# Two attention stages of a decoder step merged into one stage with a shared clock of 328 ticks

## The reference

```python
D_MODEL, SEQ, DEC_BATCH, DEC_SEQ, PAST_LEN, PAGE_SIZE = 1024, 2048, 8, 4, 4096, 128
HEAD_DIM, W_ATTN, N_HEADS_A = 64, 512, 8

def stick_breaking_block(q, k, v, bias, q_pos, k_pos):
    z = jnp.einsum('bqhd,bkhd->bhqk', q, k) * (HEAD_DIM ** -0.5) + bias[None, :, None, None]
    causal = k_pos[None, :] < q_pos[:, None]
    log_1m_beta = jnp.where(causal, jax.nn.log_sigmoid(-z), 0.0)
    tail = lax.cumsum(log_1m_beta, axis=3, reverse=True) - log_1m_beta
    w = jnp.where(causal, jnp.exp(jax.nn.log_sigmoid(z) + tail), 0.0)
    return jnp.einsum('bhqk,bkhd->bqhd', w.astype(v.dtype), v)

def attend_sample(q, k, v, bias, l=l):
    k_past = cache_k[l][page_table].reshape(n_seq_s, past_len, N_HEADS_A, HEAD_DIM)
    v_past = cache_v[l][page_table].reshape(n_seq_s, past_len, N_HEADS_A, HEAD_DIM)
    keys = jnp.concatenate([k_past, k], axis=1)
    vals = jnp.concatenate([v_past, v], axis=1)
    return stick_breaking_block(q, keys, vals, bias, past_len + jnp.arange(t_new), jnp.arange(past_len + t_new))
```

## Time and profile before

| what | us |
|---|---|
| median of three executions | 3194.71 |
| the profiled execution | 3192.91 |
| its span, first to last instruction | 3191.4 |
| prompt attention, 727.4 to 1298.2 | 570.8 |
| sample attention, 1298.2 to 1735.3 | 437.1 |

### The profile page before, as it was taken

One profiled execution on the slowest core, in us unless ns is written; L12 is line 12 of the kernel. 1 busy time (PEld: TensorE's weight loads), 2 busy tenths in 40 slices (PEclk: granted clock), 3 DMA queues, 4 the chain that ended last, 5 costly groups with the idle time before them and its releaser, 6 DMA issues. The chain is left out here.

```text
span 3191.4 us, 46062 instructions
## 1 busy us (share of the span) xinstructions
PE 2709.6 (85%) x15013; PEld 1384.8 (43%) x15013; DVE 1380.4 (43%) x2512; ACT 937.2 (29%) x1751; POOL 503.0 (16%) x678
## 2 busy tenths in 40 slices
PE   7999999977888888687776999679999999899940
PEld 3444444423444444344442455335554554455520
DVE  3141413237999999333321777612221221122237
ACT  2313030216888888222221122110100000001014
POOL 0101010100000000133332122211111111111136
PEclk9999999988999999899997999889999999999975
DMA  7020101066131510599996343378796669968637
GB/s 296 13 79 23 70 27 40 27 259 202 50 124 63 160 40 1 185 351 349 333 345 190 137 148 126 119 236 271 244 313 200 207 205 338 359 217 277 230 107 252
DMA packets 275565, 575.30 MB, mean 180 GB/s; under 512 B 59210, under 2 KB 75659, under 8 KB 271168
## 3 DMA queue, kind: packets, MB, share of 16 engines
q1 hardware_dynamic: 192620, 427.99, 38.6%
q0 software_dynamic: 82480, 145.43, 14.1%
q10 hardware_dynamic: 324, 0.10, 0.0%
HBM read 460.86 MB, written 112.29 MB: 180 GB/s over the span
## 5 line engine op out<-in xcount | busy, mean ns | idle before, releaser
L1930 PE MATMUL h<-w,xT 128*64 128x256 f32 x5120 | 590.7, 384 | 15.4 <-DMA w<-in_w 14.1
L1930 PEld LDWEIGHTS h<-w,xT 128*64 128x64 f32 x5120 | 363.9, 138 | 239.1 <-issue 70.6
L968 DVE TENSOR_TENSOR_SCAN left<-leave,left 128x512 f32<-128x512 f32 (+3 forms) x320 | 356.7, 1115 | 30.6 <-ACT leave L931 30.5
L418 PE MATMUL bank<-xnT,w_in 128*128 128x512 f32 x768 | 330.3, 592 | 0.0
L1943 PE MATMUL yb<-w,hT 128*64 128x512 f32 x1280 | 310.2, 606 | 0.0
L1010 PE MATMUL tb<-ident,w 128*128 128x128 f32 x1088 | 178.4, 288 | 88.1 <-DVE w L959 86.2
L1911 ACT ACTIVATE sg<-h 128x128 f32<-128x128 f32 x160 | 44.4, 278 | 687.0 <-PE h L1930 687.0
L1590 PE MATMUL pb<-w_out,featT 128*128 128x512 f32 x512 | 229.4, 601 | 2.3 <-DVE t L1655 2.3
L418 PEld LDWEIGHTS bank<-xnT,w_in 128*128 128x128 f32 x768 | 145.6, 190 | 181.8 <-issue 180.3
L931 ACT ACTIVATE leave<-zb,nbiasP 128x512 f32<-128x512 f32 (+3 forms) x320 | 208.4, 651 | 40.8 <-DVE w L959 27.6
L418 PE MATMUL bank<-w_in,xnT 128*128 128x512 f32 x512 | 220.4, 592 | 0.0
(11 more groups left out here) (366 smaller groups left out, 2886.9 us busy)
## 6 DMA issues: line engine op xcount, KB each, us to landing
w<-in_w SPq DMA_DIRECT2D x96, 2048.0 KB, 20.3
vp<-in_cache_v POOLq DMA_DIRECT2D x256, 256.0 KB, 5.1
w<-in_cache_k SPq DMA_DIRECT2D x256, 256.0 KB, 4.8
ys_d<-zeros SPq DMA_DIRECT2D x32, 816.0 KB
slab<-in_w_ada SPq DMA_DIRECT2D x24, 1024.0 KB, 18.3
ys_d<-y POOLq DMA_DIRECT2D x83, 256.0 KB, 10.0
x_in<-xs_d POOLq DMA_DIRECT2D x162, 128.0 KB, 6.2
w_in<-in_w_in SPq DMA_DIRECT2D x5, 2048.0 KB, 20.3
```

What stands on the lines that cost most here:

```text
L418: mm = pe.matmul(ps[:, :], w, m, start=(i == 0), stop=(i == len(parts) - 1))
L968: dve.tensor_tensor_scan(left[n % 4][:, at:at + cols][:, ::-1], leave[n % 4][:, 0:cols][:, ::-1], leave[n % 4][:, 0:cols][:, ::-1], left[n ...
L1930: mm = pe.matmul(h[half][q * G:q * G + G, 0:2 * P], xT[:, c % (XW // P), c // (XW // P) * G:c // (XW // P) * G + G], w13[i][:, c, :, cols] ...
```

## The change

`attention_phase` takes the place of both stages. PE, ACT and DVE walk one list of ticks, n = 0 to 327. At tick n PE turns item n-2 and, in the same three banks `tb`, one of 16 pieces of the sample group's K, ACT and DVE copy what was turned the tick before, ACT makes the sigmoids of item n, and DVE the product of item n-1 and the scan of item n. The sample group's units are windows of 19 ticks from tick 3: K pieces at positions 0 to 15 of a window, new positions' scores at 16, the unit's scores at 17 (in a `tb` bank), its scan at 18, the turned weights at 2 of the next window and the V products in quarters at 4, 7, 10 and 13.

In detail:
- `zb` has three banks instead of four; `tb` is shared by everything that is turned and by the sample scores; `kb` is gone.
- ACT and DVE make their copies ahead of the sigmoids and the scan of a tick, and DVE the product of n-1 ahead of the scan of n.
- The scan of an item gets its start value from a one-column copy or memset (`first`), issued after the scan of the item before; `left` is 512+1 columns, and the product is written over `take`.
- The K copies are 13 by ACT and 3 by DVE per unit, the weight copy is ACT's.
- K has two buffers of 4 pages, V two buffers of one position of all four sequences (4 pages); a V buffer is free when its quarter of products is done.
- The zero fills are issued by SP behind every second group of 4 K pages.
- `rowsS` and `rowsP` are loaded by POOL at the start of the router, since K uses their place before.

```diff
+    FIRST, WINDOW, TICKS = 3, 19, N + 8
+    def place(n):
+        return divmod(n - FIRST, WINDOW) if n >= FIRST else (-1, 0)
...
-        zb = [k.ps(f"zb{i}", [P, GRP]) for i in range(4)]
+        zb = [k.ps(f"zb{i}", [P, GRP]) for i in range(3)]
+        kp = [k.sb(f"kp{i}", [P, PPC, WA]) for i in range(2)]
+        vp = [k.sb(f"vp{i}", [P, 4, WA]) for i in range(2)]
+        kTs = [keep["rows_mem"][j // 2][:, 2 * (j % 2):2 * (j % 2) + 2, :].rearrange("p a (b n) -> p (a b) n", n=CH) for j in range(4)]
...
+                for u in range(NU):
+                    for j in range(4):
+                        g = 4 * u + j
+                        if g >= 2:
+                            turned(sp, "k_turn", (g - 2) // 4, 4 * ((g - 2) % 4) + FC - 1)
+                        page(sp, "cache_k", kp[g % 2], s_kp[g % 2], u, j)
+                        if g == 1:
+                            new_rows(0)
+                            load(1)
+                            sp.wait_ge(s_set, 1)
+                        if j == 1:
+                            zero_rows(2 * u)
+                        if j == 3:
+                            zero_rows(2 * u + 1)
...
+                for g in range(PPC * NU):
+                    u, i = divmod(g, PPC)
+                    if g >= 2:
+                        pool.wait_ge(s_spv, g - 1)
+                    for j in range(4):
+                        at = (4 * (u // NY) + j) * NPAGES + (NY - 1 - u % NY) * PPC + i
+                        number = pool.value_load(pages[0:1, at:at + 1], min_val=0, max_val=NPHYS - 1)
+                        pool.dma_start(vp[g % 2][:, j, :], cache["cache_v"][ds(number, 1)].rearrange("a p n -> (a p) n")).then_inc(s_vp[g % 2], 16)
...
+                for n in range(TICKS + 1):
+                    if n % 4 == 2 and 8 <= n < N:
+                        outputs(n // 4 - 2)
+                    if 0 <= n - 3 < N and (n - 3) % 4:
+                        turn(n - 3)
+                    u, p = place(n - 1)
+                    if p == 2 and 1 <= u <= NU:
+                        w_turn(u - 1)
+                    if p < 4 * FC and p not in (3, 7, 11) and 0 <= u < NU:
+                        k_turn(u, p)
...
+                    if n < N:
+                        pair, _, _, par, cols = item(n)
+                        head = 2 * pair + par
+                        act.wait_ge(s_z, n + 1)
+                        if n >= 4:
+                            act.wait_ge(s_sc, n - 3)
+                            turned(act, "turn", n - 4)
...
+                def first(n):
+                    _, t, c, _, cols = item(n)
+                    if n >= 4:
+                        dve.wait_ge(s_w, n - 3)
+                    if c == t // TPG:
+                        dve.memset(left[n % 4][:, cols:cols + 1], 1.0).then_inc(s_in, 1)
+                    else:
+                        dve.tensor_copy(left[n % 4][:, GRP:], left[n % 4][:, 0:1]).then_inc(s_in, 1)
+
+                def weights(n):
+                    cols = item(n)[4]
+                    dve.wait_ge(s_tk, n + 1)
+                    dve.wait_ge(s_sc, n + 1)
+                    dve.tensor_tensor(take[n % 4][:, 0:cols], take[n % 4][:, 0:cols], left[n % 4][:, 1:cols + 1], ALU.mult).then_inc(s_w, 1)
...
+                def free(*name):
+                    e = EVENT[name]
+                    if e >= 3:
+                        copied(pe, *EVENTS[e - 3][0])
+                    return bank(*name)
...
+                for n in range(TICKS):
+                    if n % 2 and n + 1 < N:
+                        scores((n + 1) // 4, (n + 1) % 4 // 2)
+                    if 2 <= n < N + 2:
+                        turn(n - 2)
...
+                    if p < 4 * FC and 0 <= u < NU:
+                        k_turn(u, p)
...
+                    if p == 17 and 0 <= u < NU:
+                        sample_scores(u)
+                    if 6 <= n < N + 6:
+                        values((n - 6) // 4, (n - 6) % 4)
+                    if p == 3 and u in (1, NY + 1):
+                        new_values(u // NY)
+                    if p in (4, 7, 10, 13) and 1 <= u <= NU:
+                        sample_values(u - 1, (p - 4) // 3)
...
+                pool.dma_start(keep["rowsS"][:, :, :], io["mod_d"][1:, :].unsqueeze(1).to_broadcast([BS, TS, 4 * D])).then_inc(s["rows"], 16)
+                pool.dma_start(keep["rowsP"][:, :, :], io["mod_d"][0:1, :].to_broadcast([P, 4 * D])).then_inc(s["rows"], 16)
...
                 dve.wait_ge(s["small"], 48)
+                dve.wait_ge(s["rows"], 32)
```

More of the change, by code:

```diff
@@ L822, in prompt_attention_phase @@
     N = 4 * M
-    LAG = 4
+    PPC = 4
+    CH = PPC * PAGE
+    NY = PAST // CH
+    NU = 2 * NY
+    FIRST, WINDOW, TICKS = 3, 19, N + 8
+    def place(n):
+        return divmod(n - FIRST, WINDOW) if n >= FIRST else (-1, 0)
+    EVENTS = []
+    for n in range(TICKS):
+        unit, p = place(n)
+        if 2 <= n < N + 2:
+            EVENTS.append((("turn", n - 2), "dve" if (n - 2) % 4 == 0 else "act"))
+        if p == 0 and unit in (1, NY + 1):
+            EVENTS.append((("new_turn", unit // NY), "dve"))
+        if p == 0 and unit in (NY + 1, NU + 1):
+            EVENTS.append((("out", unit // NY - 1), "dve"))
+        if p == 2 and 1 <= unit <= NU:
+            EVENTS.append((("w_turn", unit - 1), "act"))
+        if p < 4 * FC and 0 <= unit < NU:
+            EVENTS.append((("k_turn", unit, p), "dve" if p in (3, 7, 11) else "act"))
+        if p == 16 and unit in (0, NY):
+            EVENTS.append((("new_scores", unit // NY), "act"))
+        if p == 17 and 0 <= unit < NU:
+            EVENTS.append((("scores", unit), "act"))
+    EVENT = {name: e for e, (name, _) in enumerate(EVENTS)}
     with ExitStack() as stack:
@@ L851, in item, with turned, copied, bank @@
             return pair, t, c, par, (P * (t % TPG + 1) if c == t // TPG else GRP)
-        def columns(t, c):
-            return SEQ - P * (t + 1) + c * GRP
+        def turned(eng, *name):
+            eng.wait_ge(s_t, EVENT[name] + 1)
+        def copied(eng, *name):
+            e = EVENT[name]
+            engine = EVENTS[e][1]
+            eng.wait_ge(s_ca if engine == "act" else s_cd, sum(other == engine for _, other in EVENTS[:e + 1]))
+        def bank(*name):
+            return tb[EVENT[name] % 3]
+        def page(eng, which, dst, sem, u, j):
+            first = (4 * (u // NY) + j) * NPAGES + (NY - 1 - u % NY) * PPC
+            for i in range(PPC):
+                number = eng.value_load(pages[0:1, first + i:first + i + 1], min_val=0, max_val=NPHYS - 1)
+                eng.dma_start(dst[:, i, :], cache[which][ds(number, 1)].rearrange("a p n -> (a p) n")).then_inc(sem, 16)
         with nc.Block() as block:
@@ L1135, in _ @@
                                    pattern=[[32, 4], [TS, H]], channel_multiplier=-1)
[L1136 to L1147 removed]
+                pool.drain().then_inc(s_band, 1)
@@ L1430, in router_phase @@
         s = {n: k.sem(f"p6_{n}") for n in (
-            "w0", "w1", "wr", "small", "set", "cons",
+            "w0", "w1", "wr", "small", "rows", "set", "cons",
             "oh", "or", "oT", "fe", "hd", "mm0", "mm1", "ev0", "ev1", "x1", "xs", "xn", "xT", "xe",
```

714 lines of the change are left out of this document (299 added, 415 removed).

## The result

| what | before, us | after, us |
|---|---|---|
| median | 3195.19 (four executions, 3189.9 to 3197.31) | 3030.29 (four executions, 3027.28 to 3035.98) |
| profiled execution's span | 3191.4 | 3025.3 |
| both attentions | 1007.9 | 844.4 |
| everything behind them | 1456.1 | 1453.5 |

The ratio is 0.949 with an interval of 0.9471 to 0.951: 165 us less where 243 were forecast. The time lies in the range 2880 to 3050, but where rival (b) put it and not where my forecast did: the attention stage took 844.4 us where I had 759, and rival (b) had 804 to 884.

What follows compares the result with a forecast made beforehand. DVE bound the prompt stage and page loads the sample stage. Merged: 16 units at 44.2 us (707), plus 28, 15 and 9, gave 759 against 1007.9; with +6 in the router, 2952 us, range 2880 to 3050.

Steps and rivals of the forecast that it cites:

- rival (b): Merged stage: worse coupling makes 47 to 52 us a unit, stage 804 to 884, kernel 2997 to 3077 us; chance 0.28.
- The sums of DVE: Merged stage: prompt work plus what comes over adds to 658 us on DVE, 624 on ACT, 663 on PE.
- rival (c): V page issues on POOL starved by DVE: at 5.0 us a page, 3483 us in all, slower than before; chance 0.02.
- The forecast of 44.2 us a unit within 2.5: Each window of 19 ticks: 40.2 us of PE's work plus about 4 of coupling; 2912 to 2992 us, chance 0.52.
- late K groups: K loads landing after their buffer is needed, one named reason for 47 to 52 us a unit.
- the gap of 0.35 us between copy and product: DVE: one-column copy coming on top delays the product behind its scan; upper bound 0.35 x 320 = 112 us, 54 taken.
- the third place of the coupling: Three turned banks serve two users a tick; ACT's copy comes in time, counted nothing, else up to 0.6 us per K tick.
- PE's waits for turned banks above 50 us: Sign of error: the forecast is wrong if PE's waits for turned banks add up to more than 50 us.
- so 15, an estimate: Stage start: first K page issued behind the first queries and eight small DMAs, 15 us.
- I count 1 us a unit: K loads: at the slowest landing over a microsecond late, in two groups of a unit; 1 us a unit.
- the per-item term: PE: values 0.415, scores 0.53, four transposes 0.45, so 1.395 us for an item of 512 columns.
- The bubble at the unit's scores: Window position 17: PE makes the unit's scores in one go, so ACT and DVE lose about 2.7 us.

Runs made afterwards that it cites:

- d1: Changed kernel with the sample group's attention left out and zero fills in four lumps: 2803.65 us, ratio 0.8772; the stage 621.7 us.
- b3: Changed kernel with ACT making `leave` ahead of the copies and `take` behind them: 3004.88 us, ratio 0.9403.
- a2: Changed kernel with DVE's product of item n-1 made after the scan of item n and the one-column copy: 3093.45 us, ratio 0.9698.
- b1: Changed kernel with PE, in odd ticks, turning the item and the K piece before making the two score products: 3067.89 us, ratio 0.9607.
- b4: Changed kernel with first K pages ahead of small DMAs, query/key/value loads in three places, no zero fill in the first unit: 3009.8 us, ratio 0.9413.
- a1: Changed kernel with a prompt group's value products together in one tick instead of one block in each of four: 3027.36 us, ratio 0.949.
- c1: Changed kernel with the edits of b3 and b4 together: 2992.7 us, ratio 0.9385.
- a3: Changed kernel with two of the four transposes of each K piece left out in 15 of 16 units: 3008.58 us, ratio 0.9424.
- c3: c1 with the sample unit's scores made in two halves in two ticks, in 14 of the 16 units: 2990.85 us, ratio 0.938.
- c2: c1 with a1's edit added, value products of a prompt group together in one tick: 2981.05 us, ratio 0.9352.

## Why the prediction was right or wrong

**Right, by its own reasons.** The sums of DVE (645.7 against 658) and of ACT (603.3 against 624); the scan to product at 1.38 us (1.36), and 1.39 in d1; the wait for V pages gone (0.9 us), with the DMA engines at a share of 0.66; POOL's issue unchanged at 0.538 us, so rival (c) had no ground. 192 one-column copies of DVE ran in the stage, and no issue of V took more than 0.58 us; of the rule in the Trainium skill ("SBUF — State Buffer", "Who interferes with whom"), that DVE's two-port copies hold up POOL's descriptors, the trace shows nothing with copies this short. The router 6.0 us later.

**The range held partly by luck.** The forecast of 44.2 us a unit within 2.5 failed, and the range holds the result because it took in most of rival (b), 47 to 52 us a unit, to which I gave 0.28; it was 49.0. Of the three reasons that (b) named, late K groups came true for 16 to 20 us, the gap of 0.35 us between copy and product didn't (1.38 less 1.19 is 0.19), and PE stopped for turned banks 21.5 us in all, under the 50 that I had given as a sign. The dearest reason that was found, `leave` behind ACT's copies, isn't among them. Two other things of the expected profile were off: DVE and ACT were busy 0.76 and 0.71 of the stage, not above 0.8, and the granted clock was 0.96 on average but not above 0.95 throughout (0.50 and 0.74 in the rows at the end).

**The step that failed** is the third place of the coupling: "ACT makes that copy first in its tick, so it comes in time. I count nothing". I looked only at who waits for the copy (PE's K piece, for a bank) and not at what the copy waits for and holds up: it waits for PE's turn, 99.9 us, and `leave` stands behind it, for which DVE waits 161.7, some 90 of them in ordinary ticks. I had even given the sign of error, PE's waits for turned banks above 50 us, on the wrong side of the copy. b3 takes this cause away alone: 25 us of the median, 29 of the stage, a third of what was missing. a2 and b1, which put a delay into the ring, cost 63 and 38 us.

**Supply was under-counted.** The steps "so 15, an estimate" and "I count 1 us a unit". PE stood 8.72 us for K at the third group of the first unit, and a 6.36 us stop stood further on; I had waits "under 1 us each". I reckoned a K group's way by loads alone and let the zero fills hide; in the first unit they didn't. b4: 16 us of the stage, 20 of the median.

**PE's price was mis-sized,** but on this kernel it cost little. Values 0.59 an item instead of 0.415, turn 0.49 instead of 0.45, K piece 0.53 instead of 0.45: 0.215 x 19 + 0.08 x 16 = 5.4 us a unit more at full size, as 4-product blocks between other kinds cost more than in a row of 16 or 24. A quarter of V products took 1.00 us and a unit's scores 3.57 in fifteen of the sixteen units, so 7.6 against the 9.3 that I took: 1.7 less. With items of average size (392 us where 320 full items at 1.395 are 446, so 0.88) the first is 4.9, and the net 3.1 us a unit, about 50 in all. I had rested the per-item term on runs of like products and then set it into a tick where each stands alone. a1 shows that 28 us of PE's busy time can be taken away and that only 3 come out as time, which is no change that can be told; on c1 12 come out, and a3 gave 22 of 51. Even in a1 the sixteen products took 1.88 us and not 1.66, so 0.415 wasn't to be had in this order.

**The bubble at the unit's scores** was right as a wait: 2.7 us a unit on ACT, and 3.3 on DVE before the unit's scan. As a cost it stays open, since c3 took only a third of ACT's part away, for nothing. The forecast of 44.2 was the sum of the largest engine and two waits, without the one that b3 showed to be dear.

**What stays open.** b3, b4 and the lump take the stage from 845 to 788 us, and 759 was forecast. For the last 29 us I have no experiment; c2 still holds 41.6 us of ACT's wait for the units' scores and 14.6 us of PE's waits for K. In it PE is busy 712 of 802.6 us, ACT 598 and DVE 643, so no sum reaches the end; that three in-order engines with loads this near each other can't be kept full is an argument, not something shown. Nor do I know what halving one score block by itself would do to the changed kernel as it is, since c3 was made on c1.

## What to carry to other kernels

When a second job is woven into in-order engines, ask of each instruction both who waits for it and what stands behind it while it waits; put first what the longest ring needs (here the sigmoid before the scan), and copies after it. Price an operation by a row in which it stands alone between other kinds, if it will stand so. A wait in the profile is a cost only if taking it away moves the time: 130 us less wait gave 25 (67 came back as another wait of the same engine), 28 us less of PE's busy time gave 3, and 14 us less wait at the unit's scores gave none.

## What the runs showed of the hardware

- TensorE: four value products between transposes and scores took 0.59 us from start to start, against 1.66 for sixteen in a row (0.415 for four). In a1, in the new stage, sixteen in a row took 1.88 us (1358.49 to 1360.37). Over 1152 products their busy time fell from 183.4 to 139.8 us by putting them together, and that of PE as a whole from 756.3 to 728.1.
- A one-column copy on DVE takes its place in the gap between a scan and the product that needs it: 1.38 to 1.39 us from scan to product with it, 1.38 (1564.00 to 1565.38) without.
- TensorE's granted clock dropped after its stops. It was 0.50 (1.2 GHz) in the stage's first 20 us, in which PE was busy for 5.35, and 0.98 on average from 802.2 to 1536.8; but 0.74 in the 20 us that hold the 6.36 us stop, between two stretches at 1.00:

```profile
727.40:747.40 20.00, 5.35 (x20) 2.31 (x20) 3.24 (x16) 4.28 (x10) 7.04 (x20) 0.50 0.93 315
...
802.20:1536.80 734.60, 679.87 (x4706) 341.29 (x4704) 576.96 (x1030) 541.37 (x1060) 129.15 (x240) 0.98 0.67 222
```

```profile
967.40:987.40 20.00, 18.78 (x134) 9.49 (x134) 14.99 (x31) 15.60 (x35) 6.19 (x12) 1.00 0.96 340
987.40:1007.40 20.00, 13.61 (x81) 6.09 (x80) 12.07 (x21) 9.21 (x18) 0.54 (x1) 0.74 0.77 250
```

So a stop for supply costs twice: at 773.54, behind 8.72 us of idle time, four K transposes took 1.11 us, and mostly 0.60 to 0.66 elsewhere. It isn't only K: PE stood 1.58 us for ACT's copy before 1187.65, the clock was 0.50 from 1188 to 1191, and that unit's scores took 5.26 us instead of 3.57.
